# Value pages of a paged attention issued from SyncE's queue behind the key pages, not from ScalarE's between feature copies

## What is computed

```python
# samples (n = 8, one new token each)
past_k = cache_k[l][page_table].reshape(n_dec, past_len, A_HEADS, A_HD)
past_v = cache_v[l][page_table].reshape(n_dec, past_len, A_HEADS, A_HD)

def _diff_attend(q, k, v, q_pos, k_pos, lam):
    s = jnp.einsum('nqhmd,nkhmd->nhmqk', q, k).astype(jnp.float32) * (A_DH ** -0.5)
    mask = k_pos[None, :] <= q_pos[:, None]
    p = jax.nn.softmax(jnp.where(mask, s, -jnp.inf), axis=-1)
    p = p[:, :, 0] - lam * p[:, :, 1]
    return jnp.einsum('nhqk,nkhe->nqhe', p.astype(v.dtype), v)
```

## Time and profile before

| | us |
|---|---|
| median of 3 runs (1723.84 to 1727.78) | 1726.67 |
| span of the profiled execution, from the first to the last instruction | 1723.2 |
| feature chunk 0 (scores alone) | 57.0 |
| feature chunks 1 to 7 | 555.2 |
| feature chunk 8 (sums alone, with the scan's first preparation) | 90.9 |
| all that follows | 789.2 |
| key pages, value pages loaded | 256 each, of 256 KB |

### The profile page before, as it was taken

How to read it: one execution, slowest core, us unless ns; L and a number is a source line. 1 busy time by engine, 2 the same in 40 slices (tenths; PEclk the granted TensorE clock), 3 DMA queues, 4 the chain that set the end, 5 groups by cost and what they waited for, 6 DMA issues and landing times.

```text
span 1723.2 us, 25424 instructions
## 1 busy us (share of the span) xinstructions
PE 1485.0 (86%) x8017; PEld 855.2 (50%) x8017; DVE 872.6 (51%) x1662; ACT 308.1 (18%) x656; POOL 362.7 (21%) x262
## 2 busy tenths in 40 slices
PE   3999999798998888898978778678678587999999
PEld 3444344343443444344435567567567576455444
DVE  4446027817354453626042876877877865452100
ACT  2111010100000000000022243243243242101000
POOL 0122014514222231314012123123221320000000
PEclk8999999999999999899998799899799899988999
DMA  7021158969887897979744000100200103434121
GB/s 231 26 77 69 49 185 270 329 219 304 263 278 251 252 308 217 316 218 297 207 141 130 19 22 23 43 6 19 62 6 19 43 1 106 137 125 168 52 93 52
DMA packets 256545, 242.71 MB, mean 141 GB/s; under 512 B 22210, under 2 KB 190089, under 8 KB 256300
## 3 DMA queue, kind: packets, MB, share of 16 engines
q10 hardware_dynamic: 161200, 120.38, 22.7%
q1 hardware_dynamic: 95236, 120.96, 21.8%
HBM read 208.69 MB, written 32.79 MB: 140 GB/s over the span
## 4 chain that ended last, share of the span: by engine, by line
PE 54%; DVE 16%; DMA 10%; issue 7%; ACTq 6%; ACT 4%; POOL 2%; DVEq 0%; SPq 0%; POOLq 0%
PE ps L1540 17%; PE ps L1497 10%; PE ps L1830 6%; DMA work<-in_cache_v 6%; PE ps L1809 6%; DVE qkv L1236 5%; PE ps L1649 3%; DMA smp_dram<-sst 3%; ACTq L755 3%; ACTq L752 3%; PE ps L1560 2%; DVE sm L1181 2%; PE ps L1588 2%; ACT qkv L866 1%; PE ps L1529 1%
## 5 line engine op out<-in xcount | busy, mean ns | idle before, releaser
L1540 PE MATMUL ps<-hT,wbuf 128*128 128x512 f32 x1152 | 529.6, 615 | 0.0
L1540 PEld LDWEIGHTS ps<-hT,wbuf 128*128 128x128 f32 x1152 | 221.0, 197 | 267.4 <-issue 266.8
L1109 DVE TENSOR_REDUCE sc<-prod 128x8 f32<-128x512 f32 (+1 forms) x256 | 162.5, 674 | 34.7 <-POOL prod L605 34.7
L605 POOL TENSOR_TENSOR prod<-kbuf,qB 128x512 f32<-128x512 f32 x64 | 91.1, 1424 | 385.2 <-DMA kbuf<-in_cache_k 373.1
L1497 PE MATMUL ps<-wbuf,hT 128*128 128x512 f32 x384 | 167.1, 596 | 0.0
L776 ACT ACTIVATE fst<-ps 128x512 f32<-128x512 f32 x72 | 42.9, 595 | 544.5 <-PE ps L1540 303.7
L1649 PE MATMUL ps<-qkv,work 128*128 128x128 f32 x384 | 65.7, 325 | 62.7 <-DVE work L1303 56.7
L1809 PE MATMUL ps<-hT,wbuf 128*128 128x512 f32 x256 | 116.5, 615 | 2.8 <-ACT cos_t L940 1.6
L1497 PEld LDWEIGHTS ps<-wbuf,hT 128*128 128x128 f32 x384 | 72.9, 191 | 91.0 <-issue 90.9
L1560 PE MATMUL ps<-work,pr 128*2 128x129 f32 x2048 | 74.9, 288 | 49.7 <-DMA work<-in_cache_v 25.5
L1830 PE MATMUL ps<-qkv,work 128*128 128x512 f32 x256 | 110.3, 593 | 0.0
(11 more groups left out here) (293 smaller groups left out, 1777.1 us busy)
## 6 DMA issues: line engine op xcount, KB each, us to landing
work<-in_cache_v ACTq DMA_DIRECT2D x256, 256.0 KB, 4.1
kbuf<-in_cache_k SPq DMA_DIRECT2D x128, 256.0 KB, 5.7
work<-in_cache_k SPq DMA_DIRECT2D x128, 256.0 KB, 5.8
wbuf<-in_w_main ACTq DMA_DIRECT2D x10, 2048.0 KB, 11.5
feat_dram<-fst ACTq DMA_DIRECT2D x72, 256.0 KB, 3.7
qkv<-in_x_prompt SPq DMA_DIRECT2D x16, 512.0 KB, 4.7
vbuf<-feat_dram SPq DMA_DIRECT2D x8, 786.0 KB, 5.4
wbuf<-in_w_main SPq DMA_DIRECT2D x2, 2048.0 KB, 16.3
```

Source lines behind the costliest of these rows:

```text
L605: nc.gpsimd.tensor_tensor(prod[:, u % 4, :], kslot[u], qB[:, par, :], ALU.mult).then_inc(s["even_mul"], 1)
L1109: return nc.vector.tensor_reduce(out, v3(prod[:, u, :], 8), AX_X, ALU.add)
L1540: ins = nc.tensor.matmul(ps[:, n % 4, :], wbuf[:, wb, k, (n % 4) * P:(n % 4 + 1) * P], hT[:, k, n // 4 * W:(n // 4 + 1) * W], start=(k == ...
```

## The change

`load_v` moves from ACT's stream into SP's `pages`. In the loop over i = 1 to 3, SP issues the eight keys 8i to 8i+7 of sample j and then the eight values 8(i−1) to 8i−1 of sample j−1; values 24 to 31 follow the loop. Then come `qB` and keys 0 to 7 of sample j+1, as before. Each value still waits for `v_used` and raises the same `vin`. The call for chunk 8, which now has value pages too, moves behind the masks, the first tile and the first head.

```diff
@@ pages (SP) @@
+            def load_v(i, u):
+                vp = sp.value_load(ptab[0:1, ds((j - 1) * NPAGE + i * RING + u, 1)], min_val=0, max_val=a["cache_v"].shape[1] - 1)
+                need = reg((j - 1) * NPAGE + i * RING + (u + 1))
+                src = a["cache_v"][0, ds(vp, 1)].rearrange("o p h d -> (o p) h d")
+                sp.wait_ge(s["v_used"], need)
+                sp.dma_start(vslot[u][:, :, 0:HD], src).then_inc(s[f"vin{u // 2}"], 16)
...
-            if scores(j):
+            if scores(j) or sums(j):
                 for i in looped(sp, 1, NPAGE // RING):
-                    for u in range(RING):
+                    for u in range(RING if scores(j) else 0):
                         load_k(i, u)
+                    for u in range(RING if sums(j) else 0):
+                        load_v(i - 1, u)
+            for u in range(RING if sums(j) else 0):
+                load_v(NPAGE // RING - 1, u)
...
         bodies(sp, (), run_pages)
-        pages(8, 0, 5)
-
...
         load_tile(0, 0)
         load_head(0)
+        pages(8, 0, 5)
@@ evac_chunk (ACT) @@
-        def load_v(j, p):
-
-            vp = act.value_load(ptab[0:1, ds(j * NPAGE + p, 1)], min_val=0, max_val=a["cache_v"].shape[1] - 1)
-            src = a["cache_v"][0, ds(vp, 1)].rearrange("o p h d -> (o p) h d")
-            act.wait_ge(s["v_used"], j * NPAGE + (p + 1))
-            act.dma_start(vslot[p % RING][:, :, 0:HD], src).then_inc(s[f"vin{p % RING // 2}"], 16)
...
-                if sums(j):
-
-                    lo, hi = (0, RING) if n == 0 else [min(NPAGE, RING + (n - 2 + i) * NPAGE // 6) if n >= 2 else 0 for i in range(2)]
-                    for p in range(lo, hi):
-                        load_v(j - 1, p)
```

## The result

The changed kernel takes 1824.72 us (median; 1822.6 to 1829.41), where the kernel before took 1726.72 in the same comparison (1723.84 to 1727.78): a ratio of 1.0569, with a 95% interval of 1.054 to 1.0598. It is 98 us slower. The forecast was 1805, in a range of 1766 to 1841. The ratios leave out one execution only: of the four of the last experiment one took 2996.99 us, and no trace of it exists.

The account below looks back on a forecast made before the run. SP's issue time was taken to set chunks 1 to 7: 7 × 92 = 644 us against 555.24, +88.8, less 10 in chunk 8, together +79 on 1726.7, so 1805 us. The range was 1766 to 1841.

Parts of the forecast that it names:

- SP's turn: SP's issuing per chunk: 44.4 us of present work plus 46.1 for 32 value pages, 90.5; 92 with waiting.
- The value page: Price of one value issue on SP, start to start: 1.44 us, bounded by 1.22 and 1.54.
- The gate: SP at value page 29 waits for PE to release its slot: 0.6 to 1.9 us a chunk, 1.5 taken.
- The return of SP's loop: If SP halted at its loop's return as PE does: +12 us, 1841, used only as the range's upper end.
- Chunk 8: Without ACT's value issues the woven-in preparation comes sooner: gain 10 us, bounds 12 and 0.
- The chunk's edge: Next sample's keys 0 to 7 follow value page 31; `on` comes 4 to 5 us late, hidden behind SP's turn.
- the two stalls foreseen at 8 to 10 us: PE's waits for value pages in chunks 1 to 7, most at n=3 and n=5, 8 to 10 us each.
- Shorter landings: SP alone sends some 200 GB/s, far below 352, so pages should land sooner than the 4.1 us of before.
- rival 3: SP and PE take turns, key work at the edge uncovered: chunks of 97 to 102, 1841 to 1876 us; chance 12%.
- Rival 1: SP keeps up at 1.0 us a page and PE runs free at 66.4 a chunk: 1639 us; chance 3%.
- Rival 2: Stalls only change place, SP's issues falling into slot waits: chunks of 77 to 80, 1700 to 1727 us; chance 3%.
- The rule of the Trainium skill: Issuing from several engines saves only DMA initiation time, usually small, so giving it up would cost little: rival 1's time.

Follow-up runs that it names:

- the last experiment: Kernel with value pages 0 to 7 and chunk 8 on SP, written out (1696 us), with SP's keys held until PE has used some values: 1671.22 us.
- the early keys: Changed kernel with next sample's query and keys 0 to 7 issued ahead of value pages 24 to 31: 1824.64 us; with fixed value pages too: 1730.32 us.
- cheap issues: Changed kernel with SP's value loads taking fixed pages, without the page-table load and its register work: 1737.96 us.

## Why the prediction was right, point by point

**What bounds it.** Right. SP's turn sets the chunk; a cheaper issue shortened it with the order of transfers kept. 671.1 us stand against the 644 forecast.

**SP's turn, term by term**, in the turn of 97.17 us from 676.98 (to the next `vself` at 774.15). The 32 keys, `qB`, `kself` and `vself`: 97.17 less 32 × 1.49, 1.5 of waiting and 3.8 − 0.3 of halt leaves 44.5, for 44.4. The value page: 1.49 for 1.44, inside the bounds of 1.22 and 1.54. The gate: SP waited 16.9 us at value pages in the seven chunks, 2.4 each, for 1.5. The return of SP's loop: listed at +12 as an upper bound and not taken; it halted twice for some 3.5 more. Of the 27 us missing in chunks 1 to 7 the gate makes 6.4, the returns 7 and 224 value pages at 0.05 some 11; 2 to 3 us stay unplaced.

**Chunk 8.** The sign was right and the term too small: −10 forecast, −17.0 measured. The waits went from 90.93 − 78.07 = 12.9 to 1.1, 11.7 less; the 2 us that I kept for the tile and head loads ahead of the pages weren't needed. PE's busy time fell from 78.07 to 72.83, 5.2 less, as the granted clock rose from 0.94 to 1.00. I had counted the waits and not the slow matmuls behind them. That the total of 1805 lies only 20 us under the 1825 is in part luck: chunks 1 to 7 were 27 us too short in the forecast and chunk 8 was 7 us too long.

**The chunk's edge.** I had `on` 4 to 5 us late; the wait was 8.0 us at its longest, 30.6 in all. DVE's 27.00 us at the chunk's end became waits for key pages, 307.6 us in chunks 1 to 7. That it costs nothing here was right, and the early keys show it. That it would cost 4 to 5 us a chunk with a cheaper SP was not borne out: there the early keys were worth 1.1 at most. Of the two stalls foreseen at 8 to 10 us, the one behind n=5 came at 7.0 to 9.0 (5.88 + 1.25 + 1.83 = 9.0 in the chunk shown); the one behind n=3 was smaller than foreseen, 1.8 to 6.2 us, 4.5 in the mean.

**Shorter landings**, the reason given against rival 3, came: 4.1 to 3.4 for values, 5.7 to 3.6 for keys. The 4.1 takes in chunk 8's pages; in chunks 1 to 7 alone a value page had a median of 5.6 us before, so the fall there is larger.

```profile
work<-in_cache_v SPq DMA_DIRECT2D x256, 256.0 KB, 3.4
kbuf<-in_cache_k SPq DMA_DIRECT2D x128, 256.0 KB, 3.6
```

**The rivals.** Rival 1 had two flaws. Its condition doesn't give its time: 64 pages at 1.0 us and the 5.4 us of SP's other work make 69.4, over PE's 66.4. And it took 66.4 for granted once issues were cheap: with value pages at 0.78 and keys at 1.22, SP's own work is 69.4 too, and the chunk was 83.3. Rival 2 needed SP to spend its time at the value pages' gate; it waited 16.9 us there in seven chunks. What rival 3 describes, SP and PE waiting for each other, is seen only with cheap issues, where SP waits 96.4 us for slots; which side begins it stays open. The rule of the Trainium skill weighed in the prediction ("DMA: Bandwidth & Descriptors", "Issuing engines are not separate DMA queues") would have given rival 1's time; this kernel's runs disagree with it: the move cost 98 us.

## What to carry to other kernels

Before DMA issues move to an engine that looks idle, take the price of one from start to start in that engine's timeline, with its lookup and register work, and set the sum against the slack in its turn: here 46 us against 33. Move only what the slack holds, where it relieves the busiest engine (chunk 8's pages, and the first eight of the others), and see how the transfers then bunch: spreading them by a wait on an engine with time to spare was worth 24.7 us here, the move of the first eight 14.1 and that of chunk 8's pages some 18. A kernel's second limit shows only when the first is gone; what had next to no effect before, as half the bytes, was then worth 43 us.

## What the runs showed of the hardware that I had not expected

- What differed in the price of a DMA's issue went with its address. For the same 256 KB in 512-byte pieces: 1.49 us with a looked-up page inside a loop, 1.31 looked up but written out, 0.78 at a fixed address (always the same eight pages). The DMA instruction itself has a median of 0.54 to 0.59 in all three, so it is the work ahead of it that differs.
- SP halted for 0.8 us where its loop returned before (640.57 to 641.35), and for 3.6 and 3.8 us (758.64 to 762.43) after, with about twice the issues in the loop's body. The profile names no cause, and no run varied the body alone.
- With eight value pages on SP, written out, the DMA share stood at 1.04 to 1.10 over 30 us, with 333 to 356 GB/s; ACT's value pages issued in that burst needed 8.6 us to land, those right behind it 3.6.
- A stall of PE cost more than its length: behind the 5.88 us of wait after n=5 and the two that follow it, the next tile took 8.47 us for 7.13, and behind the 8.00 us for `on` 9.85.
